# Stick-breaking attention on one NeuronCore: a third PSUM bank for scores, written for two pieces in a row in every second step, and one bank instead of two for the sums

## What is computed

```python
def stick_breaking(q, k, v, q_pos, k_pos, bias):
    # 16 heads of 64, queries in blocks of 128
    def block(args):
        qi, pi = args
        z = jnp.einsum('bqhd,bkhd->bhqk', qi, k).astype(F32) * scale + bias_f
        mask = (k_pos[None, :] < pi[:, None])[None, None]
        log_keep = jnp.where(mask, jax.nn.log_sigmoid(-z), 0.0)
        tail = lax.cumsum(log_keep, axis=3, reverse=True)
        tail_excl = jnp.concatenate([tail[..., 1:], jnp.zeros_like(tail[..., :1])], axis=-1)
        w = jnp.where(mask, jnp.exp(jax.nn.log_sigmoid(z) + tail_excl), 0.0)
        return jnp.einsum('bhqk,bkhd->bqhd', w, v)

def sb_layer(h, pos, k_all, v_all, k_pos, w_in, q_g, bias, w_out):
    q, g = jnp.split(h @ w_in, 2, axis=-1)
    q = rmsnorm(q.reshape(B, L, SB_HEADS, SB_DH), q_g)
    o = stick_breaking(q, k_all, v_all, pos, k_pos, bias).reshape(B, L, SB_W)
    return (jax.nn.silu(g) * o) @ w_out
```

## Time and profile before

| | |
|---|---|
| median of 3 runs | 1872.53 us (1869.59 to 1873.46) |
| the profiled execution | 1870.36 us, of which 1868.5 us from its first to its last instruction |
| granted TensorE clock, mean | 0.993 of full speed |
| the attention stage | about 1360 to 1760 us from the span's start |
| PE busy in it | 378.7 of 400 us |
| DVE busy in it | 348.4 of 400 us |
| ACT busy in it | 320.5 of 400 us |

### The profile page before, as it was taken

The page is one execution under the profiler, slowest core; times in us unless marked ns, Lnnn a source line. Parts: engine busy times, 40 slices in busy tenths (PEclk is TensorE's granted clock), DMA queues, the critical chain, the costliest instruction groups (busy, mean ns, idle before and its releaser), DMA issues. The chain is left out here.

```text
span 1868.5 us, 27997 instructions
## 1 busy us (share of the span) xinstructions
PE 1801.2 (96%) x10103; PEld 1424.3 (76%) x10103; DVE 1054.1 (56%) x1975; ACT 809.0 (43%) x1682; POOL 81.0 (4%) x140
## 2 busy tenths in 40 slices
PE   4999999999999999999999999999999998999998
PEld 2678787878787878777778777888777777777677
DVE  4653535353635353633656345765168789989752
ACT  3742323232323232412345223533267678989620
POOL 2000000000000000000000000001100000000000
PEclk9999999999999999999999999999999999999999
DMA  9221212131313040583434563212342335554252
GB/s 327 85 94 58 94 58 93 58 94 56 98 52 116 35 128 22 196 275 80 136 79 169 189 217 128 83 67 89 115 113 69 94 94 175 151 150 145 61 176 96
DMA packets 184939, 215.54 MB, mean 115 GB/s; under 512 B 45352, under 2 KB 142560, under 8 KB 183809
## 3 DMA queue, kind: packets, MB, share of 16 engines
q1 hardware_dynamic: 171146, 167.17, 29.2%
q0 software_dynamic: 13696, 47.08, 6.6%
HBM read 165.39 MB, written 48.83 MB: 115 GB/s over the span
## 5 line engine op out<-in xcount | busy, mean ns | idle before, releaser
L475 PE MATMUL rt_acc<-rt_w_hi,rt_h_hi 128*128 128x512 f32 x504 | 203.3, 403 | 1.0 <-DVE rt_h_lo L1017 1.0
L477 PE MATMUL rt_acc<-rt_w_hi,rt_h_lo 128*128 128x512 f32 x504 | 197.1, 391 | 0.0
L476 PE MATMUL rt_acc<-rt_w_lo,rt_h_hi 128*128 128x512 f32 x504 | 196.5, 390 | 0.0
L1060 DVE TENSOR_TENSOR rt_by_cos<-rt_raw,rt_cos 128x256 f32<-128x256 f32 (+1 forms) x72 | 30.5, 424 | 243.8 <-ACT rt_raw L890 243.8
L901 ACT COPY rt_qk_t<-rt_tr 128x256 f32<-128x256 f32 (+1 forms) x72 | 26.0, 361 | 278.6 <-PE rt_tr L709 278.6
L2956 PE MATMUL kq_acc<-kq_w_hi,kq_h 128*128 128x512 f32 x320 | 127.1, 397 | 0.0
L2957 PE MATMUL kq_acc<-kq_w_lo,kq_h 128*128 128x512 f32 x320 | 124.8, 390 | 0.0
L2959 PE MATMUL kq_acc<-kq_w_hi,kq_h 128*128 128x512 f32 x320 | 124.7, 390 | 0.0
L477 PEld LDWEIGHTS rt_acc<-rt_w_hi,rt_h_lo 128*128 128x128 f32 x504 | 94.6, 188 | 20.6
L475 PEld LDWEIGHTS rt_acc<-rt_w_hi,rt_h_hi 128*128 128x128 f32 x504 | 94.9, 188 | 19.2 <-DVE rt_h_lo L1017 1.4
L476 PEld LDWEIGHTS rt_acc<-rt_w_lo,rt_h_hi 128*128 128x128 f32 x504 | 94.9, 188 | 17.9 <-issue 0.2
(11 more groups left out here) (414 smaller groups left out, 4160.1 us busy)
## 6 DMA issues: line engine op xcount, KB each, us to landing
ro_a_raw<-retained SPq DMA_DIRECT2D x14, 1024.0 KB, 5.9
op_ada<-in_ada_w SPq DMA_DIRECT2D x8, 1024.0 KB, 12.8
rt_w_raw<-in_ret_w_in SPq DMA_DIRECT2D x16, 512.0 KB, 5.1
rt_w_raw<-in_ret_w_in SPq DMA_DIRECT2D x8, 1024.0 KB, 7.7
rt_old<-in_state_ret SPq DMA_DIRECT2D x8, 1024.0 KB, 6.0
rt_g_raw<-in_ret_w_in SPq DMA_DIRECT2D x8, 1024.0 KB, 5.2
out_st_sample<-rt_new POOLq DMA_DIRECT2D x8, 1024.0 KB, 8.0
kq_w_raw<-in_sb_w_in SPq DMA_DIRECT2D x4, 2048.0 KB, 8.9
```

What stands on the lines that cost most here:

```text
L475: nc.tensor.matmul(dst, h_hi[:, k, cols], w_hi[:, k, :], start=k == 0, stop=False)
L476: nc.tensor.matmul(dst, h_hi[:, k, cols], w_lo[:, k, :], start=False, stop=False)
L477: last = nc.tensor.matmul(dst, h_lo[:, k, cols], w_hi[:, k, :], start=False, stop=k == KD - 1)
```

## The change

The second out bank becomes a third score bank. `scores_of(p)` picks the bank of piece p, two of the three from `z` and the third from the new tensor `pa_third`; `score(p)` waits for ACT's reading of piece p-3 instead of p-2. A list `scores_at` says which scores PE writes in which step: in an even step those of pieces p+1 and p+2, in an odd step none. It falls back to one score where the queries of piece p+2 were transposed less than two steps before. Built from the code, 76 steps have two scores, 15 have one and 77 have none. With one out bank, the first sums of a group (`opens_bank`, 15 of them) wait until DVE has read the whole group before: `out_taken` at `u // 4` instead of `u // 4 - 1`. Where this piece has both heads (7 of the 15) its sums are made one step later (`sums_at`). ACT's, DVE's and the transfers' order are as before.

```diff
-        z, wt, acc, kq, out = held.z, bank("wt", 2), bank("acc"), bank("kq"), bank("out", 2)
+        z, third, wt, acc, kq, out = held.z, bank("third"), bank("wt", 2), bank("acc"), bank("kq"), bank("out")
...
+        def scores_of(p):
+
+            return z[:, p % 3] if p % 3 < 2 else third[:, 0]
+
+        scores_at, scores_begun = [], 0
+        for p in range(NPC):
+            ahead = 1
+            if p % 2 == 0 and p + 2 < NPC:
+                at = pieces[p + 2]
+                turned = max([n for n in q_slots if at.u is not None and q_slots[n] <= at.u // QG], default=-1)
+                ahead = 2 if turned <= p - 2 else 1
+            end = min(NPC - 1, max(scores_begun, p + ahead))
+            scores_at.append(range(scores_begun + 1, end + 1))
+            scores_begun = end
+
+        def opens_bank(p):
+
+            at = pieces[p]
+            return at.closes and at.first and at.u is not None and at.u % 4 == 0 and at.u > 0
+
+        sums_at = [[] for p in range(NPC + 3)]
+        for p in range(NPC):
+            late = opens_bank(p) and len(pieces[p].heads) == 2
+            sums_at[p + (4 if late else 3)].append(p)
...
             def score(p):
                 at = pieces[p]
-                if p >= 2:
-                    pe.wait_ge(sticks, p - 1)
+                if p >= 3:
+                    pe.wait_ge(sticks, p - 2)
...
-                if at.first and at.u % 4 == 0 and at.u >= NPT:
-                    pe.wait_ge(out_taken, at.u // 4 - 1)
+                if opens_bank(p):
+                    pe.wait_ge(out_taken, at.u // 4)
...
-                        last = nc.tensor.matmul(out[hh * DH:(hh + 1) * DH, at.u // 4 % 2, t % 4 * P:(t % 4 + 1) * P], values,
+                        last = nc.tensor.matmul(out[hh * DH:(hh + 1) * DH, 0, t % 4 * P:(t % 4 + 1) * P], values,
...
             for p in range(NPC):
-                if p + 1 < NPC:
-                    score(p + 1)
+                for n in scores_at[p]:
+                    score(n)
                 if p in q_slots:
                     turn_q(q_slots[p])
...
-                if p >= 3:
-                    attend(p - 3)
+                for n in sums_at[p]:
+                    attend(n)
...
-                nc.vector.tensor_tensor(dst, out[:, u // 4 % 2, :], own, ALU.mult).then_inc(out_taken, 1)
+                nc.vector.tensor_tensor(dst, out[:, 0, :], own, ALU.mult).then_inc(out_taken, 1)
```

More of the change, by code:

```diff
@@ L1729, in score @@
                         for j in range(GR):
-                            last = nc.tensor.matmul(z[GW * j:GW * (j + 1), p % 2, 0:NK], sa.q_diag[:, at.b, 2 * j + e, :],
+                            last = nc.tensor.matmul(scores_of(p)[GW * j:GW * (j + 1), 0:NK], sa.q_diag[:, at.b, 2 * j + e, :],
                                                     sa.k_t[:, at.b % 2, 2 * j + e, :], start=e == 0, stop=e == 1, tile_position=(0, GW * j))
@@ L1744, in score @@
                 for i, hh in enumerate(at.heads):
-                    dst, keys = z[:, p % 2, i * n:(i + 1) * n], k_t[:, pair % 2, hh, c0:c0 + n]
+                    dst, keys = scores_of(p)[:, i * n:(i + 1) * n], k_t[:, pair % 2, hh, c0:c0 + n]
                     nc.tensor.matmul(dst, q_hi[:, g % 2, hh, at.u % QG, :], keys, start=True, stop=False)
@@ L1873, in _ @@
             turn_w(NPC - 2)
-            attend(NPC - 3)
+            for n in sums_at[NPC]:
+                attend(n)
             turn_w(NPC - 1)
-            attend(NPC - 2)
-            attend(NPC - 1)
+            for n in sums_at[NPC + 1] + sums_at[NPC + 2]:
+                attend(n)
             pe.wait_ge(next_loaded, 16)
@@ L1921, in stick @@
                     act.wait_ge(w_turned, p - TR + 1)
-                dst, src = (keep[:, p % 2, 0:n], take[:, p % TR, 0:n]), z[:, p % 2, 0:n]
+                dst, src = (keep[:, p % 2, 0:n], take[:, p % TR, 0:n]), scores_of(p)[:, 0:n]
                 if len(at.heads) == 2:
```

## The result

The changed kernel takes 1875.32 us (median of 20 runs) against 1871.83 us for the kernel before it (20 runs): a ratio of 1.0020 (1.0013 to 1.0027). It is slower, by some 3.5 us. The profiled execution took 1870.06 us, almost what that of before took; a single execution doesn't tell 3 us, as the opening and the clock differ from one to the next. The views after are read like the earlier trace rows. First busy time in stretches: length, then each engine's busy us (PE, PEld, DVE, ACT, POOL), granted clock, DMA.

A forecast was written before the change was run, and what follows sets the result against it. In the attention stage PE and DVE were taken to set the pace in turn. Half of 1.9 + 0.7 + 5.7 (4.15) less half of 1.5 + 0.9 + 0.2 (1.3) gave a 2.9 us gain: median 1869.6 us, range 1862 to 1876.5.

The forecast's parts named there:

- a rival to which it gave 0.13: Attention stage: transposes behind two scores reach ACT and DVE 0.5 us late, 5.4 us slower, 1877.9 us; chance 0.13.
- The score that moves forward moves other work back: Even steps: transposes and sums behind two scores come 0.5 us later, costing 1.5 us before half is passed on.
- The waits for a score bank: PE ahead of scores: nearly all of its 10.6 us waiting for ACT goes, worth 5.7 us before half is passed on.
- The exchange: Odd steps: transposes instead of a score behind sums save 0.04 us at 48 places, 1.9 us before half is passed on.
- the exchange itself saves nothing: Rival: transposes behind sums cost the 0.10 us a score costs there, leaving a 1.9 us gain, 1870.6 us; chance 0.10.
- Three blocks of sums are fewer: Sums moved a step at pieces 40, 80 and 124 merge with the next piece's, saving 0.7 us before halving.
- The small part of the queries: Second scores of even steps: an added wait for DVE's write, 0.6 us at step 36, 0.9 us in all before halving.
- One out bank: Sums that open a bank: an added wait for DVE's reading, 0.2 us in all before halving, upper bound 5 us.
- Nothing is passed on: Rival: DVE sets the pace, PE's gain turns into waits for DVE's product, time stays 1872.5 us; chance 0.15.

The follow-up runs named there:

- one score a step: The changed kernel with its third score bank, single out bank and later sums, but one score in every step: 1869.18 us (0.9993) and 1871.03 us (0.9995).
- one out bank alone: The kernel before with one bank for sums, its wait and the later sums, two score banks in the old order: 1871.67 us, 1.0004.
- pairs both behind: The changed kernel with both scores of a step moved behind the transposes of the weights: 1873.85 us, 1.0020.
- the 25 pairs: The changed kernel with two scores only in steps that transpose nothing into pa_kq, 25 of 76 such steps staying: 1871.76 us, 1.0012.

## Why the prediction was wrong

It forecast a gain of 2.9 us and a slowdown of 3.5 us was measured, inside the range (1862 to 1876.5), by the mechanism of a rival to which it gave 0.13.

**The step that failed: "The score that moves forward moves other work back".** It counted 0.5 us of lateness at half of the 12 places where DVE waits for ACT's factors, 3 us, took the middle of nothing and that, 1.5, and passed on half. Measured is 3.5 us in the stage between one score a step (-1.6) and pairs (+1.9). Three things were left out. First, one of the two scores may be a sample piece's, 16 products. Second, what ACT reads next behind its sigmoids is the copy from `pa_kq`, and only then the weights. Third, DVE waits for PE's work directly too, for some turned weights and for the sums of the sample groups. Step 120 shows the first two. PE and ACT in the changed kernel:

```profile
1652.45 0.39 PE L1771 MATMUL z<-pa_k_t,pa_q_hi 128*128 128x256 f32 x1
...
1653.52 1.28 PE L1755 MATMUL pa_third<-sa_k_t,sa_q_diag 128*32 128x320 f32 x16
1654.74 0.66 PE L1741 MATMUL pa_kq<-ident,sa_k_pages 128*128 128x128 f32 x4
1655.23 0.60 PE L1786 MATMUL pa_wt<-ident,pa_take 128*128 128x128 f32 x4
```

```profile
1655.43 0.59 ACT L1990 COPY sa_k_t<-pa_kq 128x512 f32<-128x512 f32 x1 [1.70 <-PE pa_kq L1741]
1655.91 0.59 ACT L1969 COPY pa_w_t<-pa_wt 128x512 f32<-128x512 f32 x1
1656.39 0.61 ACT L1950 ACTIVATE pa_keep<-z 128x512 f32<-128x512 f32 x1
```

```profile
1657.04 0.69 DVE L2083 TENSOR_TENSOR_SCAN pa_after_key<-pa_keep 128x256 f32<-128x256 f32 x1 [1.20 <-ACT pa_keep L1950]
```

The transposes into pa_kq begin 2.29 us behind the first score. ACT stands 1.70 us for them, its sigmoids of the next piece follow the two copies, and DVE stands 1.20 us for the sigmoids. With one score a step the same transposes stand ahead of the sample's score:

```profile
1653.17 0.38 PE L1771 MATMUL z<-pa_k_t,pa_q_hi 128*128 128x256 f32 x1
...
1654.15 0.61 PE L1741 MATMUL pa_kq<-ident,sa_k_pages 128*128 128x128 f32 x4
```

```profile
1654.79 0.59 ACT L1990 COPY sa_k_t<-pa_kq 128x512 f32<-128x512 f32 x1 [0.54 <-PE pa_kq L1741]
```

0.98 us behind the first score, and ACT waits 0.54 us. This place alone costs DVE 0.8 us. Six places, at pieces 48, 117, 121, 127, 141 and 145, cost 0.4 to 0.8 us each against one score a step, 3.8 in sum, the same in all three executions of the changed kernel; smaller ups and downs make the rest. At 121, 127 and 141 (1.8 us) the lateness goes from pa_kq over ACT to DVE, as here. At the other three (2.0 us) DVE itself waits for PE, at 48 for turned weights that DVE copies, at 117 and 145 for the sums of a sample group. DVE's rows at 48, 117 and 145 in the changed kernel:

```profile
1486.77 0.42 DVE L2102 COPY pa_w_t<-pa_wt 128x256 f32<-128x256 f32 x1 [0.59 <-PE pa_wt L1786]
...
1647.39 0.42 DVE L2127 TENSOR_TENSOR sa_o_own<-pa_acc,sa_own_block 128x256 f32<-128x256 f32 x1 [0.47 <-PE pa_acc L1835]
...
1710.45 0.42 DVE L2127 TENSOR_TENSOR sa_o_own<-pa_acc,sa_own_block 128x256 f32<-128x256 f32 x1 [0.64 <-PE pa_acc L1835]
```

With one score a step none of these three waits is there. The rival decided from fewer places than the 8 it named, since it, too, was priced at 0.5; and it, too, named only the way over ACT.

**The waits for a score bank: "nearly all of the 10.6 us goes".** Wrong: 8.5 us stay. Counted once it is worse: 8.0 of 8.1 us. (The prediction read the 10.6 us and the 9.6 us as PE's waits; they hold some of them twice. PE found the product not ready 14 times, not 21.) Of the 17 waits 14 stand ahead of a second score. Only the first score of a pair waits for an older piece. The second, of piece p+2 in step p, waits for ACT's reading of piece p-1, which is what the score of step p waited for before; half a microsecond of the first score ahead of it doesn't cover that. The third bank removes the wait only with one score a step (1.1 us left). There it is worth 1.4 us (-1.6 against -0.2 with one out bank alone), where I counted 5.7 and half of it passed on: even a wait that goes is worth a quarter of what was read as its worth, as PE's wait for DVE's product takes its place (16.0 us in that kernel, 9.6 before; counted once 10.2 and 6.6).

**The exchange: "saves 0.10 - 0.06 = 0.04 us".** Wrong, in the term for the score. PE's timeline with pairs: a second score, and later transposes behind sums. Then the kernel with one score a step: a score behind sums, and transposes behind the score.

```profile
1668.45 0.44 PE L1771 MATMUL pa_third<-pa_k_t,pa_q_hi 128*128 128x512 f32 x1
1668.73 0.40 PE L1775 MATMUL pa_third<-pa_k_t,pa_q_lo 128*128 128x512 f32 x1
...
1669.78 0.44 PE L1814 MATMUL pa_out<-pa_w_t,pa_v 128*64 128x128 f32 x4
1670.15 0.66 PE L1786 MATMUL pa_wt<-ident,pa_take 128*128 128x128 f32 x4
1670.64 0.53 PE L1844 MATMUL pa_acc<-sa_by_group,sa_o_own 128*128 128x32 f32 x4
```

```profile
1669.30 0.50 PE L1771 MATMUL pa_third<-pa_k_t,pa_q_hi 128*128 128x512 f32 x1
1669.63 0.39 PE L1775 MATMUL pa_third<-pa_k_t,pa_q_lo 128*128 128x512 f32 x1
...
1669.92 0.60 PE L1786 MATMUL pa_wt<-ident,pa_take 128*128 128x128 f32 x4
1670.37 0.53 PE L1844 MATMUL pa_acc<-sa_by_group,sa_o_own 128*128 128x32 f32 x4
```

Sums of 4 take 0.37 us to the next row also ahead of transposes, as forecast. Four transposes then take 0.49 us (1670.15 to 1670.64) in place of 0.45 (1669.92 to 1670.37), also nearly as forecast: over the stage the first transpose behind sums takes 0.06 us more than elsewhere (median of 47). But the prediction took the price of the moved score from one behind gate products, 0.24 us, and in a pair it stands behind another score. There its first product takes 0.28 us (1668.45 to 1668.73), behind sums 0.33 (1669.30 to 1669.63); the medians of the stage are 0.28 and 0.34. So 0.06 us is saved and 0.06 paid, and the exchange is worth nothing where 1.9 us were forecast. This is what the rival "the exchange itself saves nothing" had. Three blocks of sums are fewer (92, from 95), as forecast.

The rule of the Trainium skill that changing the tiling mode drains the engine (TensorEngine Tiling (Array Packing), Key Properties) makes it 0 as well. The trace agrees: from the last row of sums to the next row it is 0.20 us ahead of scores and of transposes alike (medians), and the first row is 0.06 us longer in either case.

**The small part of the queries**: the wait of step 36 came, 0.92 us (0.6 forecast), and four more, ahead of the second scores 46, 78, 124 and 166, of 0.25 to 1.25 us; the five are 3.9 us, where 0.9 was forecast. Their own cost in the stage wasn't separated from the pairs'.

**One out bank**: "0.2" was right, 0 measured. That the later sums are what makes it so, 8 to 9 us in the stage with the stretches at 1.2 GHz in it, was not seen.

**"Nothing is passed on"** was half right: PE's wait for the product did grow (14.4, forecast 13 or more), and PE's busy time from DVE's product of piece 16 to the last fell from 332.8 to 330.1 us for nothing (330.0 and 328.7 in the other two executions). It is 329.0 us with one score a step, so the fall doesn't come from the pairs.

**The remaining 1.6 us.** The stage explains 1.9 of 3.5 us. The mean granted clock of all runs was 0.9893, 0.9896 and 0.9904 in the changed kernel's three jobs, 0.9907 to 0.9916 in before's; among before's runs of one job those at 0.990 took 1.8 to 3.3 us more than those at 0.992. A straight line of time over clock, fitted to the runs of a job with the same slope for both kernels (1.1 to 1.6 us for each 0.001), gives an estimate of the difference at equal clock: the changed kernel is 1.3 us slower (0.7 to 1.9) in its second job and 1.2 (0.4 to 2.0) in its third, of 4.0 and 2.7 us between the means. That fits the stage's 1.9, so about half of the 3.5 us goes with the lower clock. The same estimate is -1.7 and -1.2 us for one score a step, +5.8 for pairs in odd steps, -3.1 and -2.8 for two banks with the score behind the weights, and where the stage's figure has a stretch at half clock in it, it is lower: +1.7 in place of 3.7 for pairs both behind, +0.5 in place of 3.0 for the 25 pairs, +2.6 in place of 6.2 for one score without the later sums. In two of its three profiles the clock falls inside the stage (this is of the first; in the earlier trace rows' kernel the same stretch has 1.00):

```profile
1535.00:1540.00 5.00, 5.00 (x32) 3.91 (x32) 4.79 (x7) 4.35 (x10) 0.60 (x1) 0.66 0.97 315
```

At that place it costs nothing: the third execution, without it, has the same times there within 0.1 us. In other executions it may fall elsewhere. The lower clock is measured and the time goes with it; why the changed kernel's clock is lower stays open.

## What to carry to other kernels

Where an engine's program feeds two others in turn, read what each step puts ahead of the piece that they wait for next, all of it and at its largest, not at its mean: a lump of two in one step and none in the next makes every second hand-over later, time is lost where its reader stands waiting, and little of it is won back at the early ones. List every reader of the moved work, not only the next in the chain. Before adding a buffer, try the order: moving one score behind the transposes won 0.1% and 0.3% in two jobs with the old banks, and the third bank then added nothing. When a wait is to go, check which event the moved instruction still waits for.

## What the hardware showed that was not expected

The granted clock fell to 1.2 GHz inside the stage (1380 to 1750 us) in 6 of 9 profiled executions of kernels with pairs, in none of the 10 of kernels with one score a step and the old or the later sums, and twice in the one without the later sums. Each of these nine stretches was 3.4 to 10.2 us long and began close to a place at which PE had stood for 1.5 to 2.2 us: 1.57 ahead of 1565.62 in the kernel with 25 pairs, down at 1566.1; 2.24 ahead of 1476.92 in the one without the later sums, down at 1476.1. But waits as long also stand in the kernels in which it didn't fall (1.57 us at 1565.33 in the kernel before), so PE's wait is not enough to bring it about. Where PE was on the path, a stretch of 3.4 us cost 1.5 to 1.8 us; at 1536 us it cost nothing.
